# Layer 0's expert stage: first block's rows listed from the ranks, two modulation units moved to the stage's tail

## The chip, the cores and the metric

The kernel runs on one core of one Trainium2 chip, in float32. The metric is device time of one execution in microseconds (us). TensorE (PE, with PEld its weight load), VectorE (DVE), ScalarE (ACT), GpSimd (POOL) and SyncE (SP, which here only issues DMAs) run side by side, each through its own list of instructions in order, and meet at semaphores.

## What is computed

Two model blocks stand one behind the other. The change touches only the first, which has two layers over 512 tokens and 256 context tokens, and in it the end of layer 0: a mixture of experts with 32 experts, two of them chosen for each of the 768 rows, and the modulation vectors with which layer 1 begins.

```python
for layer in range(DEPTH):
    sh1, sc1, g1, sh2, sc2, g2 = jnp.split((silu_c @ mod_w[layer] + mod_b[layer])[:, None, :], N_MOD, axis=-1)
    ...
    h = rmsnorm(x, norm_mix_g[layer]) * (1.0 + sc1) + sh1
    ...
    h2 = rmsnorm(x, norm_ffn_g[layer]) * (1.0 + sc2) + sh2
    ...
        out = hier_moe(jnp.concatenate([h2.reshape(b * s, d), hc2.reshape(-1, d)], axis=0), *moe)
        x = x + g2 * out[: b * s].reshape(x.shape)
```

`hier_moe` picks a group, then two experts in it, sorts the rows by expert, computes `(silu(x @ w_gate[e]) * (x @ w_up[e])) @ w_down[e]` for each expert's rows and adds the weighted results back.

## The kernel before

**One block for each expert.** The 32 experts are given to 32 blocks by rank of their row count. A narrow block holds 64 rows, a wide one 128 (in layer 0 the blocks 7, 14, 21, 26, 4 and 10). Each needs three weight matrices (gate, up, down) of 128 x 4096 float32, 2 MB each. They go round in eight slots: six parts of `ring`, one in `hT`, one in `scr`. Blocks 0 and 1 are always experts of fixed number, so SP can load their weights with plain DMAs before the ranks are known (`fixed` in `sp_moe`); POOL fetches the others with indirect DMAs (`pool_blocks`) whose row numbers stand in `wix`. Should an expert have more rows than its block, further blocks follow in a general path (`further`), which in these runs is branched over.

**The router's stage.** PE multiplies by the router's weights (`pe_router`), DVE finds the two experts of each row, counts, and computes from them where every row goes (`dve_router`). Meanwhile PE transposes the 768 rows of h, ACT copies them to SBUF and POOL writes them as six tiles to `hrows` in DRAM. Then PE turns places into lists (`pe_router_rows`, `pe_router_halves`): for each block the 128 row numbers (`rt`), and where its results go (`rw`, `rn`). DVE signals `order` when the experts' order stands in `wix`, `rt` and `rows` when the lists stand, and `ox` after the tables of the general path and the weights w1, w2. POOL waits for the rows out, for `rt`, gathers the rows of blocks 0 to 2 from `hrows`, waits for `rows`, fetches block 2's gate, waits for `ox`, and then goes through the blocks: rows of b+3, up of b+2, down of b+1, gate of b+3, results of b-1 (to `yrows`). A fetch into a slot waits until PE has done with what was in it.

**Modulation of the next layer.** Units 0 to 3 of layer 1's modulation (2 MB of `mod_w` each) are computed inside layer 0's router stage. SP loads each in two halves of 1 MB into ring slot 0 (`mod_load`); a half waits until PE has done with the half before in its place. PE makes 8 matmuls for a unit (`pe_mod_pieces`), ACT copies the result (`mod_row`), PE turns it into columns (`pe_mod_turn`), ACT copies these (`mod_columns`), and DVE adds the bias. Slot 0 is also the place of block 1's gate, so `fixed(1, 0)` waits for unit 3.

**Layer 1's stage** has no modulation units and already works in another way: DVE makes from block 0's column of the ranks a table `first_oa`, PE multiplies it with the row numbers ("r_0", 4 matmuls there), and `first_rt` lists block 0's rows. POOL gathers them at once, and `pe_router_rows` and `pe_router_halves` stand within block 0's matmuls (`among`, behind steps 2 and 5 of 8).

**The tail.** SP loads the results of six tiles of 128 rows (1 MB each) from `yrows` once all are written, here into ring slots 0 to 2 (`moe_y`). Per tile ACT scales by w1 (`weigh`), DVE and POOL add the second expert's half, PE transposes (`turn`), DVE adds to x (`add`), ACT squares (`squares`), PE sums the squares (`sums`), ACT copies (`groups`), PE makes the total (`total_columns`). Behind it come the root, the reciprocal and layer 1's first scaling.

Of the kernel before, what the change touches and what calls it, by code (L numbers as in the profile page):

```python
# [8 lines left out]
ALU = mybir.AluOpType  # L9
# [17 lines left out]
FIXED = 2  # L27
# [248 lines left out]
def build(nc, I, out, upto=99):  # L276
# [67 lines left out]
    FURTHER_SLOTS = (0, 1, 5, IN_H, IN_SCRATCH, 2)  # L344
# [780 lines left out]
    def expert_slot(kind, b):  # L1125

        if b >= 32:
            return FURTHER_SLOTS[(3 * (b - 32) + kind) % 6]
        read = min(3 * b + 4, 95) if kind == 2 and b < 32 else 3 * b + 4 if kind == 2 else 3 * b - 1 + kind if b else kind
        return EXPERT_SLOTS[read % 8]  # L1130
# [8 lines left out]
    def sp_moe(e, l):  # L1139
# [22 lines left out]
        for u in (1, 2, 3):  # L1162
            mod_load(u)
        fixed(1, *((0, 1) if l == 1 else (1,)))
# [4 lines left out]
        if l == 0:  # L1169
            e.wait_ge(*ps.filled("mod", 1, 3))  # L1170
            fixed(1, 0)
# [29 lines left out]
    def pe_router(e, l):  # L1201
# [45 lines left out]
        if l == 0:  # L1247
            rows(3)
        else:
            o = ps.take("r_0", l)  # L1250
            e.wait_ge(*ps.ready("r_0", l))
            e.wait_ge(*dve_step.of(l, "first_oa"))
            for i in range(NT):
                m = e.matmul(o[:, 0:1], M.first_oa[:, 128 * i:128 * i + 128], k("tok")[:, i:i + 1], i == 0, i == NT - 1)
            m.then_inc(*ps.fill("r_0", l))
# [4 lines left out]
        if l == 0:  # L1260
            for i in range(4, NT):
                rows(i)
# [30 lines left out]
    def act_router(e, l):  # L1293
# [19 lines left out]
        if l == 0:  # L1313
            mod_columns(e, M.mod, 0)
            mod_row(e, M.mod, 2)
            mod_columns(e, M.mod, 1)
            mod_row(e, M.mod, 3)
            mod_columns(e, M.mod, 2)
            mod_columns(e, M.mod, 3)
# [9 lines left out]
    def dve_router(e, l):  # L1329
# [49 lines left out]
        if l == 1:  # L1379
            e.wait_ge(*ps.filled("r_k", l))  # L1380
            rank_in = ps.ap("r_k", l)[:, 0:32 * NT].rearrange("p (t e) -> p t e", e=32)
            chosen = M.AA.rearrange("p (t e) -> p t e", e=32)
            go(e.stt(M.first_key, rank_in[:, :, 0], 1.0, chosen[:, :, 0], ADD, MUL))
            e.stt(M.first_oa.rearrange("p (t s) -> p t s", s=128), M.spread[:, None, :].broadcast_to([128, NT, 128]), 1.0,
# [2449 lines left out]
```

## Time and profile before

| | us |
|---|---|
| median of 3 runs | 2998.05 |
| lowest, highest | 2992.88, 2999.28 |
| the profiled execution: its time | 2988.78 |
| the profiled execution: its span | 2987.0 |
| in it: layer 0's router stage | 288 to 346 |
| in it: layer 0's blocks | 346 to 839 |
| in it: layer 0's tail | 839 to 876 |

All times "at" a point are us from the span's start. The profiled execution is 9.3 us (0.31%) below the median. In a row of the timeline the first number is the start, the second the length, and in brackets stands how long the engine was idle before it and what ended that.

### The profile page before, as it was taken

What the parts mean: (1) busy time and instruction counts of PE and PEld (TensorE: products, weight loads), DVE (VectorE), ACT (ScalarE), POOL (GpSimd) and SP (SyncE); (2) the same over time, 40 slices, a digit from 0 to 9 for tenths busy, and PEclk for the clock granted to TensorE, in tenths of its full rate; (3) what the DMA queues carried; (4) which work ended last, traced back from release to release, by engine and by line L of the source; (5) the groups of instructions that cost most, each with busy time, mean ns of one, the idle gap of its engine ahead of it and who ended that gap; (6) DMA issues with size and microseconds to landing.
All of it is one profiled execution on the core that took longest, in us unless ns stands there. A gap on an engine that the chain in (4) does not pass through costs nothing.

```text
span 2987.0 us, 36438 instructions
## 1 busy us (share of the span) xinstructions
PE 2810.7 (94%) x15530; PEld 1917.0 (64%) x15530; DVE 1045.0 (35%) x2088; ACT 754.0 (25%) x1311; POOL 515.5 (17%) x519
## 2 busy tenths in 40 slices
PE   7989899999979999989999989999999889999997
PEld 4778456544548765745355537888865557888876
DVE  5983300000053343330000016242285554432334
ACT  4142311111142154311111114222111264321223
POOL 0000133332220044133332311000043140000000
PEclk9999899999989999989999999999999999999998
DMA  8612999999942132389999983232311201322321
GB/s 294 200 46 90 385 425 427 426 426 426 412 166 73 57 127 85 122 339 426 426 426 426 426 342 124 87 111 85 127 36 45 103 1 63 117 94 94 99 90 45
DMA packets 142537, 621.51 MB, mean 208 GB/s; under 512 B 15698, under 2 KB 96722, under 8 KB 108704
## 3 DMA queue, kind: packets, MB, share of 16 engines
q0 software_dynamic: 42336, 403.76, 32.1%
q1 hardware_dynamic: 98880, 210.35, 20.4%
q10 hardware_dynamic: 1152, 4.98, 0.5%
q8 instruction: 127, 2.08, 0.3%
q14 instruction: 42, 0.34, 0.0%
HBM read 624.26 MB, written 26.74 MB: 218 GB/s over the span
## 4 chain that ended last, share of the span: by engine, by line
PE 77%; DMA 11%; DVE 5%; ACT 3%; issue 2%; POOL 1%; SPq 1%; DVEq 0%; POOLq 0%; ACTq 0%
PE ps L92 75%; DMA ring<-in_exp_up,wix 7%; PE ps L95 2%; DVE scr L114 2%; ACT hT L98 1%; SPq L132 1%; DMA hT<-in_exp_up,wix 1%; DMA scr<-in_exp_up,wix 1%; DVE xT L114 1%; DMA ring<-in_mod_w 1%; POOL scr L110 0%; DVE scr L117 0%; POOL yrows L139 0%; ACT ring L102 0%; DVE scr L106 0%
## 5 line engine op out<-in xcount | busy, mean ns | idle before, releaser
L92 PE MATMUL ps<-ring_r 128*128 128x512 f32 (+1 forms) x2688 | 772.6, 374 | 6.1 <-DVE hT_r L106 4.0
L92 PEld LDWEIGHTS ps<-ring_r 128*128 128x128 f32 x2688 | 492.7, 190 | 114.0 <-issue 18.3
L92 PE MATMUL ps<-ring,scr 128*64 128x512 f32 (+4 forms) x2176 | 461.2, 548 | 19.4 <-DMA ring<-in_exp_up,wix 14.4
L92 PE MATMUL ps<-hT_r,ring_r 128*128 128x512 f32 (+1 forms) x1256 | 470.0, 374 | 0.0
L92 PEld LDWEIGHTS ps<-ring,scr 128*64 128x64 f32 (+2 forms) x2176 | 163.8, 141 | 223.6 <-issue 210.4
L92 PE MATMUL ps<-scr_r,ring_r 128*128 128x512 f32 x1312 | 306.7, 390 | 0.3 <-issue 0.3
L106 DVE TENSOR_TENSOR scr<-scr,ps 64x512 f32<-64x512 f32 (+1 forms) x76 | 52.5, 691 | 661.4 <-ACT scr L98 498.2
L92 PEld LDWEIGHTS ps<-scr_r,ring_r 128*128 128x128 f32 x1312 | 246.2, 188 | 52.4 <-issue 0.5
L92 PEld LDWEIGHTS ps<-hT_r,ring_r 128*128 128x128 f32 x1256 | 238.4, 190 | 41.2 <-issue 0.5
L92 PE MATMUL ps<-ring,hT 128*64 128x512 f32 (+3 forms) x992 | 247.3, 539 | 16.4 <-DMA ring<-in_exp_up,wix 12.6
L106 DVE TENSOR_TENSOR ring_r<-ring,ring_r 128x2048 fp32r<-128x2048 f32 (+1 forms) x102 | 225.0, 2229 | 89.5 <-ACT ring_r L102 89.2
L102 ACT ACTIVATE ring_r<-ring 128x2048 fp32r<-128x2048 f32 (+1 forms) x102 | 186.5, 1836 | 184.4 <-DMA ring<-in_ffn_w 132.0
L98 ACT ACTIVATE scr<-ps 64x512 f32<-64x512 f32 (+2 forms) x96 | 55.9, 583 | 603.1 <-PE ps L92 603.1
L92 PEld LDWEIGHTS ps<-ring,hT 128*64 128x64 f32 (+1 forms) x992 | 111.4, 166 | 121.9 <-issue 109.3
L92 PEld LDWEIGHTS ps<-KC,scr 128*128 128x128 f32 x1168 | 148.7, 201 | 62.2 <-issue 37.5
L102 ACT ACTIVATE scr<-ps 128x512 f32<-128x512 f32 (+2 forms) x178 | 91.1, 522 | 370.7 <-PE ps L92 367.5
L92 PE MATMUL ps<-KC,scr 128*128 128x64 f32 (+2 forms) x1168 | 156.9, 282 | 23.3 <-DVE scr L106 13.4
L92 PE MATMUL ps<-scr 128*32 128x128 f32 (+5 forms) x712 | 144.5, 409 | 7.9 <-DMA ring<-in_exp_up,wix 3.1
L92 PE MATMUL ps<-ring 128*64 128x128 f32 (+10 forms) x904 | 134.7, 400 | 17.1 <-ACT scr L102 10.1
L103 DVE COPY scr<-ps 128x512 f32<-128x512 f32 (+3 forms) x94 | 46.1, 500 | 290.1 <-PE ps L95 173.6
L92 PE MATMUL ps<-hT,ring 128*32 128x62 f32 (+2 forms) x1088 | 138.6, 316 | 9.2 <-issue 9.2
L106 DVE TENSOR_TENSOR scr<-hT,ps 128x512 f32<-128x512 f32 x44 | 30.2, 687 | 310.3 <-PE ps L92 310.3
(169 smaller groups left out, 2920.0 us busy)
## 6 DMA issues: line engine op xcount, KB each, us to landing
ring<-in_ffn_w SPq DMA_DIRECT2D x66, 1024.0 KB, 5.5
ring<-in_mod_w SPq DMA_DIRECT2D x12, 2048.0 KB, 8.5
ring<-in_mod_w SPq DMA_DIRECT2D x24, 1024.0 KB, 5.7
ring<-in_exp_up SPq DMA_DIRECT2D x4, 2048.0 KB, 11.0
ring<-in_exp_down SPq DMA_DIRECT2D x4, 2048.0 KB, 9.4
ring<-in_exp_gate SPq DMA_DIRECT2D x4, 2048.0 KB, 12.4
ring<-in_w_in SPq DMA_DIRECT2D x4, 2048.0 KB, 8.2
ring<-in_w_cd SPq DMA_DIRECT2D x6, 1024.0 KB, 6.0
```

Source lines behind the costliest of these rows:

```text
L92: return self.real.matmul(o, l, r, start=start, stop=stop) if self.real else Quiet()
L95: return self.real.transpose(o, i, identity) if self.real else Quiet()
L98: return self.real.activation(o, i, f, **how) if self.real else Quiet()
L102: return self.real.activation(o, i, ACT.Copy) if self.real else Quiet()
L103: return self.real.tensor_copy(o, i) if self.real else Quiet()
L106: return self.real.tensor_tensor(o, a, b, op) if self.real else Quiet()
L114: return self.real.scalar_tensor_tensor(out=o, in0=a, scalar=s, in1=b, op0=op0, op1=op1) if self.real else Quiet()
L132: return self.real.dma_start(o, i) if self.real else Quiet()
```

## The change

- Layer 0 also makes `first_oa` and `first_rt` from the ranks (6 matmuls on PE, four operations on DVE); POOL gathers block 0's rows right behind the rows' writes and then fetches block 2's gate at `order`; the lists are made within block 0's matmuls.
- Units 2 and 3 leave the router's stage. Block 1's gate, up are loaded when unit 1 is through.
- The tail's six tiles land in `hT` (2), `scr` (2) and ring slot 2 (2). Units 2 and 3 are loaded whole into ring slots 0 and 1, behind the tail's rows on SP. PE computes them behind tile 4's sums, ACT copies them ahead of tile 5's squares, and DVE's bias and gains stand at the stage's end.
- The general path goes round four slots in place of six.

On SP in layer 0's router stage and behind it (`in_mod_w` 128x2048 is half a unit, 128x4096 a whole one; `w_cd` belongs to layer 1):

```order
 L132 DMA ring<-in_exp_gate 128x4096
-L132 DMA ring<-in_mod_w 128x2048 x6
+L132 DMA ring<-in_mod_w 128x2048 x2
+L132 DMA ring<-in_exp_gate 128x4096
 L132 DMA ring<-in_exp_up 128x4096
-L132 DMA ring<-in_exp_gate 128x4096
 L132 DMA ring<-in_exp_down 128x4096
 L132 DMA ring<-in_w_cd 128x8x256
 L132 DMA ring<-in_w_cd 128x8x128 x2
-L132 DMA ring<-yrows 128x2x1024 x6
+L132 DMA hT<-yrows 128x2x1024 x2
+L132 DMA scr<-yrows 128x2x1024 x2
+L132 DMA ring<-yrows 128x2x1024 x2
+L132 DMA ring<-in_mod_w 128x4096 x2
```

Four half units are gone ahead of the blocks, and two whole units stand behind the six row loads.

On POOL at the start of layer 0's blocks (`scr<-hrows` gathers a block's rows), before:

```order
L132 DMA hrows<-scr 128x1024 x2
L132 DMA hrows<-ring 128x1024 x4
L135 DMA scr<-hrows,scr 128x1024 x3
L135 DMA hT<-in_exp_gate,wix 128x4096
L135 DMA scr<-hrows,scr 128x1024
L135 DMA scr<-in_exp_up,wix 128x4096
```

and in the changed kernel:

```order
L132 DMA hrows<-scr 128x1024 x2
L132 DMA hrows<-ring 128x1024 x4
L135 DMA scr<-hrows,scr 128x1024
L135 DMA hT<-in_exp_gate,wix 128x4096
L135 DMA scr<-hrows,scr 128x1024 x3
L135 DMA scr<-in_exp_up,wix 128x4096
```

Block 2's gate moved ahead of the rows of blocks 1 and 2; the three gathers behind it and block 2's up now wait for lists that PE makes within block 0.

On ACT at the end of the tail (`hT<-xT` are the squares of a tile, `scr<-ps 128x128` the groups), before:

```order
L98 ACTIVATE hT<-xT 128x1024
L102 ACTIVATE scr<-ps 128x128
L98 ACTIVATE hT<-xT 128x1024
L102 ACTIVATE scr<-ps 128x128 x2
L98 ACTIVATE stat<-ps,KC 128x6
```

and in the changed kernel:

```order
L98 ACTIVATE hT<-xT 128x1024
L102 ACTIVATE scr<-ps 128x128
L102 ACTIVATE scr<-ps 128x512 x2
L98 ACTIVATE hT<-xT 128x1024
L102 ACTIVATE scr<-ps 128x128
L102 ACTIVATE MT<-ps 128x8 x2
L102 ACTIVATE scr<-ps 128x128
L98 ACTIVATE stat<-ps,KC 128x6
```

The copies of units 2 and 3 stand ahead of the last tile's squares, the copies of their columns ahead of its groups.

The diff, cut to what the prediction speaks of:

```diff
-    FURTHER_SLOTS = (0, 1, 5, IN_H, IN_SCRATCH, 2)
+    FURTHER_SLOTS = (5, IN_H, IN_SCRATCH, 2)
...
         mod_load(0)
         fixed(0, 0)
-        for u in (1, 2, 3):
-            mod_load(u)
-        fixed(1, *((0, 1) if l == 1 else (1,)))
+        mod_load(1)
+        if l == 0:
+            e.wait_ge(*ps.filled("mod", 1, 1))
+        fixed(1, 0, 1)
...
         e.wait_ge(*xg_in[0].of(l, 0))
-        if l == 0:
-            e.wait_ge(*ps.filled("mod", 1, 3))
-            fixed(1, 0)
         fixed(1, 2)
...
+        for u in (2, 3) if l == 0 else ():
+            weights_load(e, u - 2, ("mod", 1, u), I["mod_w"][1, u], 8, 512)
...
-            pe_mod_pieces(e, 2)
             pe_mod_turn(e, M.mod, 1)
-            pe_router_rows(e, l)
-            pe_mod_pieces(e, 3)
-            pe_router_halves(e, l)
-            pe_mod_turn(e, M.mod, 2)
-            pe_mod_turn(e, M.mod, 3)
...
-        among = {2: pe_router_rows, 5: pe_router_halves} if l == 1 and first == 0 else {}
+        among = {2: pe_router_rows, 5: pe_router_halves} if first == 0 else {}
...
-        if l == 1:
-            e.gather(M.xr[0], hrows, M.first_rt, bounds_check=767, oob_is_err=False).then_inc(*xg_in[0].up(l, 0, by=16))
-            e.wait_ge(*dve_step.of(l, "order"))
-            fetch(FIXED, 0)
+        e.gather(M.xr[0], hrows, M.first_rt, bounds_check=767, oob_is_err=False).then_inc(*xg_in[0].up(l, 0, by=16))
+        e.wait_ge(*dve_step.of(l, "order"))
+        fetch(FIXED, 0)
         e.wait_ge(*dve_step.of(l, "rt"))
-        for b in range(l, 3):
+        for b in (1, 2):
             fetch_x(b)
-        if l == 0:
-            e.wait_ge(*dve_step.of(l, "rows"))
-            fetch(FIXED, 0)
         e.wait_ge(*dve_step.of(l, "ox"))
...
         if l == 0:
-            return ring[:, a:a + 2048]
+            return hT[:, a:a + 2048] if i < 2 else scr[:, a - SLOT:a - SLOT + 2048] if i < 4 else ring[:, a:a + 2048]
...
+        if l == 0:
+            for u in (2, 3):
+                pe_mod_unit(e, M.mod, u)
+            for u in (2, 3):
+                pe_mod_turn(e, M.mod, u)
         sums(M.NT - 1)
...
+            if l == 0 and i == M.NT - 1:
+                mod_row(e, M.mod, 2)
+                mod_row(e, M.mod, 3)
             squares(i)
             if i:
                 groups(i - 1)
+        if l == 0:
+            mod_columns(e, M.mod, 2)
+            mod_columns(e, M.mod, 3)
         groups(M.NT - 1)
...
-        if l == 0:
-            dve_mod_bias(e, M.mod)
-            e.wait_ge(*dve_step.of("mod_b", M.mod.name))
-            dve_gains(e, "at_in", 1, 0, "nmix")
-        else:
+        if l == 1:
             dve_two_gains(e)
```

## Rows read from the trace of the kernel before

**Rows 1.** The page's chain that ended last, by engine.
```profile
PE 77%; DMA 11%; DVE 5%; ACT 3%; issue 2%; POOL 1%; SPq 1%; DVEq 0%; POOLq 0%; ACTq 0%
```

**Rows 2.** Windows: length, PE, PEld, DVE, ACT, POOL busy, PE clock, DMA share, GB/s.
```profile
310.00:330.00 20.00, 15.53 (x126) 11.07 (x125) 16.41 (x62) 9.19 (x19) 3.52 (x6) 1.00 0.83 292
343.00:356.00 13.00, 12.31 (x46) 5.44 (x45) 0.00 (x0) 1.88 (x2) 1.94 (x2) 0.65 1.00 423
372.00:600.00 228.00, 228.00 (x1344) 131.60 (x1344) 20.16 (x34) 26.43 (x45) 72.83 (x75) 1.00 1.01 426
600.00:818.00 218.00, 204.34 (x1124) 105.16 (x1122) 17.36 (x30) 24.99 (x42) 63.15 (x65) 0.98 1.01 424
1302.00:1309.00 7.00, 6.65 (x46) 3.62 (x44) 3.95 (x15) 1.19 (x2) 4.43 (x5) 1.00 0.28 80
```

**Rows 3.** Chain of waits in layer 0's blocks: start, length, what.
```profile
602.41 12.55 PE ps L92 x64
...
619.10 29.06 DMA ring<-in_exp_up,wix
...
794.90 26.92 DMA hT<-in_exp_up,wix
```

**Rows 4.** Timeline of SP and POOL, layer 0's router stage.
```profile
313.35 0.33 SPq L132 DMA_DIRECT2D ring<-in_mod_w  x1
...
335.33 1.09 POOL L135 DMA_INDIRECT scr<-hrows,scr  x1 [9.04 <-DVE scr L106]
...
347.92 0.95 POOL L135 DMA_INDIRECT scr<-in_exp_up,wix  x1 [0.30 <-issue]
```

**Rows 5.** Timeline of POOL, the same place in layer 1.
```profile
1286.83 1.18 POOL L135 DMA_INDIRECT scr<-hrows,scr  x1 [8.77 <-DMA hrows<-ring]
...
1307.25 0.95 POOL L135 DMA_INDIRECT scr<-in_exp_up,wix  x1 [0.30 <-issue]
```

**Rows 6.** Landing of POOL's DMAs issued at 325.8, 1277.5, 360.3, 1311.1.
```profile
DMA to landing us min/median/max: 4.9/4.9/4.9
...
DMA to landing us min/median/max: 8.4/8.4/8.4
...
DMA to landing us min/median/max: 14.1/14.1/14.1
...
DMA to landing us min/median/max: 16.5/16.5/16.5
```

**Rows 7.** Timeline, router lists: PE and DVE in layer 0, then in layer 1.
```profile
328.65 1.83 DVE L106 TENSOR_TENSOR scr<-scr 128x768 f32<-128x768 f32 x2
329.75 3.65 PE L92 MATMUL ps<-scr 128*128 128x49 f32 x24 [1.20 <-DVE scr L106]
335.25 0.72 DVE L117 TENSOR_REDUCE scr<-scr 128x17 f32<-128x544 f32 x1
...
1298.85 1.98 PE L92 MATMUL ps<-scr 128*128 128x43 f32 x16
1302.45 0.52 DVE L117 TENSOR_REDUCE scr<-scr 128x11 f32<-128x352 f32 x1
```

**Rows 8.** The tail's six row loads on SP: issue, and landing.
```profile
L132 SPq DMA_DIRECT2D ring<-yrows x6: 396/516/1060, 843.0 to 846.5; - x6
...
DMA to landing us min/median/max: 6.5/11.6/15.8
```

**Rows 9.** Timeline: unit and turn in the router stage, then the tail's end.
```profile
325.64 1.92 PE L92 MATMUL ps<-ring,scr 128*32 128x512 f32 x16
327.50 1.05 PE L92 MATMUL ps<-AM,scr 128*128 128x2 f32 x8
338.45 0.60 ACT L102 ACTIVATE scr<-ps 128x512 f32<-128x512 f32 x1 [9.69 <-PE ps L92]
...
869.93 1.06 ACT L98 ACTIVATE hT<-xT 128x1024 f32<-128x1024 f32 x1 [0.84 <-DVE xT L114]
871.04 1.08 PE L92 MATMUL ps<-hT,KC 128*32 128x128 f32 x16 [1.02 <-ACT hT L98]
872.05 1.11 PE L92 MATMUL ps<-AM,scr 128*128 128x1 f32 x4
873.92 2.93 PE L92 MATMUL ps<-KC,stat 128*128 128x128 f32 x12 [0.76 <-DVE stat L120]
```

**Rows 10.** Windows at the tail's end, columns as in Rows 2.
```profile
871.00:877.50 6.50, 5.70 (x34) 4.66 (x34) 1.54 (x4) 1.31 (x4) 0.00 (x0) 0.50 0.00 0
```

More of the change, by code:

```diff
@@ L1127, in expert_slot @@
         if b >= 32:
-            return FURTHER_SLOTS[(3 * (b - 32) + kind) % 6]
+            return FURTHER_SLOTS[(3 * (b - 32) + kind) % 4]
         read = min(3 * b + 4, 95) if kind == 2 and b < 32 else 3 * b + 4 if kind == 2 else 3 * b - 1 + kind if b else kind
@@ L1246, in pe_router @@
         e.matmul(o[:, 0:32], k("tri"), M.AA[:, 0:32], True, True).then_inc(*ps.fill("r_k", l))
-        if l == 0:
-            rows(3)
-        else:
[L1250 to L1255, printed above, removed]
+        for i in (3, 4) if l == 0 else ():
+            rows(i)
+        o = ps.take("r_0", l)
+        e.wait_ge(*ps.ready("r_0", l))
+        e.wait_ge(*dve_step.of(l, "first_oa"))
+        for i in range(NT):
+            m = e.matmul(o[:, 0:1], M.first_oa[:, 128 * i:128 * i + 128], k("tok")[:, i:i + 1], i == 0, i == NT - 1)
+        m.then_inc(*ps.fill("r_0", l))
         o = ps.take("r_p", l)
@@ L1260, in pe_router @@
         if l == 0:
-            for i in range(4, NT):
-                rows(i)
+            rows(5)
             pe_mod_turn(e, M.mod, 0)
-            pe_mod_pieces(e, 2)
             pe_mod_turn(e, M.mod, 1)
-            pe_router_rows(e, l)
-            pe_mod_pieces(e, 3)
-            pe_router_halves(e, l)
-            pe_mod_turn(e, M.mod, 2)
-            pe_mod_turn(e, M.mod, 3)
     def pe_router_rows(e, l):
@@ L1378, in dve_router @@
         go(e.reduce(place, cmp, ADD))
-        if l == 1:
[L1380 to L1384, printed above, removed]
-                  bc(M.first_key[:, :, None], 128), ADD, ALU.is_equal).then_inc(*dve_step.up(l, "first_oa"))
+        e.wait_ge(*ps.filled("r_k", l))
+        rank_in = ps.ap("r_k", l)[:, 0:32 * NT].rearrange("p (t e) -> p t e", e=32)
+        chosen = M.AA.rearrange("p (t e) -> p t e", e=32)
+        go(e.stt(M.first_key, rank_in[:, :, 0], 1.0, chosen[:, :, 0], ADD, MUL))
+        e.stt(M.first_oa.rearrange("p (t s) -> p t s", s=128), M.spread[:, None, :].broadcast_to([128, NT, 128]), 1.0,
+              bc(M.first_key[:, :, None], 128), ADD, ALU.is_equal).then_inc(*dve_step.up(l, "first_oa"))
         go(e.ts(cap, rank, WIDES[l] + 0.5, ALU.is_le, 64.0, MUL))
@@ L1396, in dve_router @@
         go(e.ts(rows[:, 128:160], p32(k("iota"))[:, 0:32], p32(k("p")), ALU.is_ge, ov, MUL), l, "by_expert")
-        if l == 1:
-            e.wait_ge(*ps.filled("r_0", l))
-            v = ps.ap("r_0", l)[:, 0:1]
-            go(e.ts(M.first_z, v, 0.5, ALU.is_le, 65536.0, MUL))
-            e.stt(M.first_rt, v, -1.0, M.first_z, ADD, ADD).then_inc(*ps.empty("r_0", l))
+        e.wait_ge(*ps.filled("r_0", l))
+        v = ps.ap("r_0", l)[:, 0:1]
+        go(e.ts(M.first_z, v, 0.5, ALU.is_le, 65536.0, MUL))
+        e.stt(M.first_rt, v, -1.0, M.first_z, ADD, ADD).then_inc(*ps.empty("r_0", l))
         e.wait_ge(*ps.filled("r_p", l))
@@ L1906, in dve_moe @@
         add(M.NT - 1)
+        if l == 0:
+            dve_mod_bias(e, M.mod)
+            e.wait_ge(*dve_step.of("mod_b", M.mod.name))
+            dve_gains(e, "at_in", 1, 0, "nmix")
         stage_end(e, f"m{l}", "act", "pe")
@@ L1913, in pool_moe @@
         e.wait_ge(*rows_out[1].of(l, M.NT - 1))
-        if l == 1:
-            e.wait_ge(*ps.emptied("r_0", l))
+        e.wait_ge(*ps.emptied("r_0", l))
         pool_blocks(e, l)
```

7 lines of the change are left out of this document (removed).

## The prediction

> **What bounds the kernel now.** Start with the chain of waits: 77% of the span is PE's and 11% DMA's [rows 1], so the first reading is that PE decides. In order of time layer 0's blocks look like that too, up to 615; behind it the chain changes to waits for expert weights of 27 to 29 us each [rows 3]. The reader should then turn to the windows, since a chain that runs over PE does not say that the DMA engines had time to spare. From 343 to 818 their share is 1.00 to 1.01 at 423 to 426 GB/s, whether PE waits or not [rows 2]. So the stream of weights is what ends layer 0's blocks. PE has only been given a start by the weights of blocks 0 and 1, and has used it up at 615. The last fetches make it plain: the up weights issued at 794.90 take 26.92 us to land, of which their own 2.10 MB need 2.10/0.426 = 4.92 us; the rest is queue [rows 2, 3]. The time of layer 0's blocks is therefore: the moment from which the stream runs without holes, and what is still to be moved from there. PE's own start is no term as long as the queue stays full. In the tail no DMA queue is full any more; there the last tile's chain from DVE over ACT and PE counts [rows 9].
>
> **The change, part 1: the stream's start.** Removed ahead of the blocks are units 2 and 3, 4.19 MB, worth 4.19/0.426 = 9.8 us of DMA time. What matters is whether holes open instead. I follow the new order.
>
> Block 1's gate and up are issued where unit 2's second half is now, at 313.4 [rows 4], in place of later. That is 4.19 MB, and with the six tiles of `hrows` (3.15 MB) 7.34 MB. At 426 GB/s they take 17.2 us. With some 2 us until the first bytes move (an estimate: half a megabyte alone takes 4.9 us, 1.2 of it bytes [rows 6]) the last row write lands near 313.4 + 2 + 17.2 = 332.6; the stretch ran at 292 GB/s with a share of 0.83, that is 352 at a full share, so I add 0.7: 333.3. The rows' last write itself is hardly moved: `first_oa` (768 columns, 0.92 us [rows 7]) and its matmuls delay the last transposes by a few tenths. The ends: it lands 4.9 us after its issue at 325.8 as now, 330.7; or 8.4 us after as in layer 1, and a bit more for the bigger backlog, 335 [rows 6].
>
> From there layer 1 is the model, because it has this very order. Its last row write lands at 1277.5 + 8.4 = 1285.9 and block 2's up is issued at 1307.25 [rows 5, 6], 21.3 us later: gather of block 0's rows, its transposes, three steps of block 0, the lists, `rt`, the rows of blocks 1 and 2, `ox`, the rows of block 3. Layer 0 has 24 passes for the lists where layer 1 has 16 at 0.124 us (1.98 us), +1.0; and `ox` runs over 17 further blocks instead of 11 in two operations, 0.72 against 0.52 us, +0.4 [rows 7]. So 22.7 us, and the up weights of block 2 go out at 333.3 + 22.7 = 356.0 instead of 347.92 [rows 4]. Before that time POOL has only block 2's gate to fetch and SP only block 1's down, and both have landed by about 348. The DMA engines then run nearly empty, as in layer 1, whose window 1302 to 1309 has a share of 0.28 [rows 2]. The hole eats the 9.8 us.
>
> The balance is read where both stages do the same again, block 3's up. In layer 1 it lands at 1311.1 + 16.5 = 1327.6, 20.3 us after the issue at 1307.25 [rows 5, 6]. Here: 356.0 + 20.3 = 376.3. Now it lands at 360.3 + 14.1 = 374.4 [rows 6]. Behind it the same 86 fetches follow in both kernels. **The stream ends 1.9 us later**; with the ends of the row write -0.7 to +3.6.
>
> What is moved on PE, DVE and ACT here costs nothing of its own: units 2 and 3 (1.92 us each at full clock [rows 9]) leave a stretch in which PE waits for DMA and DVE anyway, and PE reaches block 1 some 2 us earlier than now (an estimate: block 0's rows arrive some 4 us earlier, but the lists, 3 us, stand within its matmuls). That only makes the queue of fetches longer. If the queue were not full, it would be a gain (a rival, below).
>
> **Part 2: the tail.** The six tiles are issued from 843.0 to 846.5, and the last lands 15.8 us after its issue, at 862.3 [rows 8]. The two units are next in SP's queue: 862.3 + 2 x 4.92 = 872.1 for unit 3. All times in this part are those of before; part 1 shifts them together. PE needs 1.92 us for a unit: unit 2 is there early enough and is computed from 870.0, unit 3 is done at 874.1. ACT copies it (0.60, until 874.7), and only then, being in order, squares the last tile, which it now starts at 869.93 although its input is there. Queued behind the waiting ACT instruction is all that the end of the stage needs; who waits for it is PE's last sums. PE meanwhile makes unit 3's turn (1.05, until 876.2 with unit 2's), so the sums that now start at 871.04 start at 876.2 [rows 9]. At full clock they and the last total take some 1.3 us, with ACT's copy between them: 877.5, against 873.2 now (872.05 + 1.11). That is +4.3. One part comes back: sums, totals and roots now run at the level of 0.50, 1.2 GHz, because PE had waited 1.02 us for ACT behind a thin stretch [rows 9, 10]; with the units in that place I expect the 2.4 GHz level to be kept, and the first 8 of 12 root passes (2.93 x 8/12 = 2.0 us) to take half. **+3.4 us**, from +2.5 (unit 3 lands a microsecond earlier) to +9 (clock low, below). DVE's bias and gains (two short operations) are done while ACT and PE make the last total. The landing places in `hT` and `scr` change no length. The third `w_cd` load lands some 10 us later (4.19 MB more ahead of it); it is layer 1's third piece of weights, and PE takes it up only behind two others, so I count it as covered. The general path isn't run; four slots cost nothing.
>
> The Trainium skill, page "TensorE: Matmul & The Clock Gate" (Part 1), says that the throttled state is the default and that activity releases it. By that rule PE's added work before 871 keeps the higher level; the trace of before only shows the fall behind PE's wait, so it does not decide this.
>
> A second rule bears on part 1. The rows show a half-megabyte write of layer 1 landing 8.4 us after its issue while SP's 2 MB loads are ahead of it. The Trainium skill, page "DMA: Bandwidth & Descriptors" (Queues, rings and completion order), says that each DMA engine takes turns between the queue rows, packet by packet. By turns, the last row write would be through once its queue's share is, about a microsecond sooner than with all loads ahead of it, and the stream would end about 1 us later instead of 1.9.
>
> **The sum:** 1.9 + 3.4 = 5.3 us. The profiled execution took 2988.78, so 2994.1; it lies 9.3 us under the median of the three runs, so as a median 2998.05 + 5.3 = **3003.4**.
>
> **Rivals.**
> - **The stream banks all of its 4.19 MB (faster).** Block 2's up would have to be issued when block 1's down lands, near 347, so that no hole opens. Then the stream ends 9.8 us earlier, and with the tail's 3.4 the kernel takes 2991.6. It decides at the issue of that fetch: each microsecond before 354.1 is gained. For it speaks that POOL's first gather comes about 1 us earlier than now (333.3 + 0.9 against 335.33 [rows 4]); against it, that `ox` hangs on block 0's matmuls, and layer 1's hole [rows 2].
> - **PE's chain decides.** If the queue of fetches is not what ends the blocks, PE's earlier start, about 2.2 us, is the gain: -2.2 + 3.4, 2999.3. For it speaks the chain up to 615 [rows 3], against it the share of 1.01 in the same stretch [rows 2].
> - **The low clock in the tail.** If the level falls at 871 as now, units and turns cost double: the two units end at 870.0 + 7.7 = 877.7, turns near 881, the total near 882: +8 to +9 in place of 3.4, 3009. Now the low level holds until 877.5 [rows 10].
> - **The moved units are hidden.** Units 2 and 3 would have to land before 868; they are behind 6.3 MB of rows, so only another order of landing gives it. Price 0 for the tail: 3000.
>
> **Chances.** Forecast 0.50; stream banks 0.11; PE's chain 0.17; low clock 0.16; hidden 0.06. A measurement of this kernel can tell about 0.2%, 6.0 us, from no change. The forecast lies at 5.3 and its own range is 2999 to 3008, so I count 0.22 of its 0.50 as slower and 0.28 as same; low clock is slower (0.15); half of the first rival is faster (0.06), with 0.03 for starts that I have not seen. Faster 0.09, same 0.53, slower 0.38. The range is 2991 to 3011: from the first rival to low clock with the late row write.
>
> **What would show it.** In the trace of after: the last row write lands near 333; block 0's gather behind it by 1 us; block 2's up issued near 356 (this decides part 1); a window of low DMA share from 348 to 357; block 3's up lands near 376; from there all transfers shifted by 2 us; in the tail unit 3's matmuls wait for DMA until 872 plus the shift, ACT's squares of the last tile start near 875 plus the shift, and PE's clock is 1.00 there. I am wrong if the window near 350 is full, if the last up lands earlier than now, or if squares are not late.

## The result

| | before | after |
|---|---|---|
| median, lowest to highest (10 runs each) | 2993.62 (2988.20 to 2999.28) | 3002.76 (2997.61 to 3009.56) |
| the profiled execution: time, span | 2988.78, 2987.0 | 3000.24, 2998.5 |
| first scaling of layer 1 in it | 876.11 | 883.53 |

All in us. The changed kernel is slower: ratio 1.0031, 95% interval 1.0023 to 1.0040, that is 9.3 us (6.9 to 12). The three runs shown ahead of the prediction had a median of 2998.05; with ten it is 2993.62. In the two profiles the stage of the change ends 7.4 us later. The rest of the gap of 11.5 us between the two spans arises in code that the change doesn't touch (see the last section).

The profile after. The page's chain of waits by engine, against [rows 1]:

```profile
PE 70%; DMA 12%; ACT 2%; issue 2%; DVE 2%; POOL 1%; DVEq 0%; SPq 0%; POOLq 0%; ACTq 0%
```

Windows of the changed kernel; the columns are those of [rows 2] (the last two numbers are the DMA share and GB/s, ahead of them the PE clock):

```profile
300.00:330.00 30.00, 26.53 (x172) 17.33 (x170) 20.40 (x73) 14.94 (x30) 3.51 (x6) 0.88 0.85 334
330.00:345.00 15.00, 4.58 (x20) 4.00 (x21) 1.93 (x3) 1.48 (x3) 2.09 (x2) 0.50 0.71 268
345.00:365.00 20.00, 18.99 (x102) 9.38 (x100) 5.43 (x20) 1.76 (x3) 6.85 (x7) 0.88 0.57 211
...
350.00:360.00 10.00, 9.33 (x67) 6.04 (x67) 5.00 (x19) 0.68 (x2) 3.45 (x4) 1.00 0.21 62
...
372.00:600.00 228.00, 228.00 (x1346) 131.59 (x1342) 20.21 (x34) 26.21 (x44) 72.42 (x75) 1.00 1.01 426
```

And the same three first stretches of the kernel before:

```profile
300.00:330.00 30.00, 23.64 (x178) 14.16 (x177) 20.23 (x70) 15.42 (x31) 3.52 (x6) 1.00 0.89 338
330.00:345.00 15.00, 13.82 (x74) 10.24 (x73) 5.14 (x20) 0.95 (x3) 4.06 (x4) 0.55 0.99 395
345.00:365.00 20.00, 19.02 (x85) 7.69 (x85) 1.12 (x2) 3.07 (x4) 4.82 (x5) 0.82 1.01 429
```

This is the reading that decides the case. Before, the DMA engines are busy all the time from 330; after, they stand nearly still from 350 to 360, and are idle for about three tenths of 330 to 345. From 372 the stream is full in both kernels, so hardly anything behind it can make the hole good (about a microsecond was, see the prediction's steps). A stream that always ends the stage may be accounted like money: share times length is the time for which the engines were busy. From 300 to 380 the kernel before uses 76.9 us of full share, the changed one 62.7 us. It loses 14.2 us, has 9.8 us less to move, and should end 4.4 us later. The chain of waits of the changed kernel, against [rows 3], shows its last fetches:

```profile
621.70 31.52 DMA ring<-in_exp_up,wix
...
797.42 28.71 DMA hT<-in_exp_up,wix
...
852.07 23.73 DMA ring<-in_mod_w
```

Start plus length is the landing: the one issued at 797.42 lands at 826.13, before at 794.90 + 26.92 = 821.82. That is 4.3 us later, as the account says. The third row is new: the tail now ends on the landing of unit 3.

Why the hole is there, from POOL's timeline after, against [rows 4]:

```profile
328.25 0.53 POOL L132 DMA_DIRECT2D hrows<-ring  x1 [4.65 <-ACT ring L102]
336.58 1.09 POOL L135 DMA_INDIRECT scr<-hrows,scr  x1 [7.80 <-issue]
337.98 1.00 POOL L135 DMA_INDIRECT hT<-in_exp_gate,wix  x1 [0.30 <-issue]
354.38 1.00 POOL L135 DMA_INDIRECT scr<-hrows,scr  x1 [15.41 <-DVE scr L103]
...
359.55 0.95 POOL L135 DMA_INDIRECT scr<-in_exp_up,wix  x1 [0.30 <-issue]
```

POOL waits 15.41 us for the lists (DVE's copy into `scr`), with only block 2's gate in its queue, which landed at 349.4; SP has only block 1's down, landed at 352.0. Block 2's up, which before went out at 347.92, goes out at 359.55. What POOL waits for is on PE:

```profile
325.96 1.12 PE L95 MATMUL ps<-KC,hT 128*128 128x128 f32 x4 [1.46 <-DVE scr L106]
...
344.38 5.39 PE L92 MATMUL ps<-ring,hT 128*64 128x512 f32 x12 [0.73 <-issue]
349.69 2.96 PE L92 MATMUL ps<-scr 128*128 128x49 f32 x24
```

The lists (x24) stand behind 5.39 us of block 0's matmuls, which run at the low level behind a wait of 9.68 us for block 0's rows (the window 330 to 345 has a clock of 0.50, and so has 326 to 330 ahead of the wait); the next 12 take 2.80. The first row shows a smaller thing: the last transposes of h wait 1.46 us for DVE, since they take the PSUM bank in which the ranks stood. DVE in turn makes `first_oa` (0.96 us) ahead of the sums for PE's next product. So the last row write goes out at 328.25 and not at 325.77. Whether that costs anything is tested below ("The last transposes").

The tail after, PE and then ACT and DVE, against [rows 9]:

```profile
873.17 1.92 PE L92 MATMUL ps<-ring,scr 128*32 128x512 f32 x16
875.84 1.92 PE L92 MATMUL ps<-ring,scr 128*32 128x512 f32 x16 [0.75 <-DMA ring<-in_mod_w]
877.70 1.95 PE L92 MATMUL ps<-AM,scr 128*128 128x2 f32 x16
879.57 0.65 PE L92 MATMUL ps<-hT,KC 128*32 128x128 f32 x16
...
881.82 2.46 PE L92 MATMUL ps<-KC,stat 128*128 128x128 f32 x12 [0.76 <-DVE stat L120]
```

```profile
877.83 0.60 ACT L102 ACTIVATE scr<-ps 128x512 f32<-128x512 f32 x1 [2.08 <-PE ps L92]
878.33 1.05 ACT L98 ACTIVATE hT<-xT 128x1024 f32<-128x1024 f32 x1
...
883.53 2.97 DVE L114 SCALAR_TENSOR_TENSOR hT<-xT,AM,ps 128x512 f32<-128x512 f32 x5 [1.77 <-PE ps L92]
```

Unit 3's matmuls wait for its landing (875.80), ACT copies it, and only then makes the squares of the last tile. From the first row load to the first scaling the tail takes 883.53 - 847.04 = 36.5 us, before 876.11 - 843.04 = 33.1: 3.4 us more. Its PE clock is 1.00 where [rows 10] had 0.50:

```profile
871.00:877.50 6.50, 4.98 (x54) 1.80 (x53) 2.11 (x9) 1.82 (x3) 0.00 (x0) 1.00 0.91 338
```

### The profile page after: what moved, and what is told of

It is laid out like the page before. It is cut to its first block, busy times and chain, and to the rows that moved or that the text cites. A ratio compares the mean times of both kernels' runs of the same rounds, so it can differ in the third digit from the quotient of the medians.

```text
span 2998.5 us, 36465 instructions
## 1 busy us (share of the span) xinstructions
PE 2812.2 (94%) x15542; PEld 1918.3 (64%) x15542; DVE 1046.8 (35%) x2092; ACT 755.1 (25%) x1311; POOL 516.9 (17%) x519
## 3 DMA queue, kind: packets, MB, share of 16 engines
q1 hardware_dynamic: 98592, 210.35, 20.3%
## 4 chain that ended last, share of the span: by engine, by line
PE 70%; DMA 12%; ACT 2%; issue 2%; DVE 2%; POOL 1%; DVEq 0%; SPq 0%; POOLq 0%; ACTq 0%
PE ps L92 67%; DMA ring<-in_exp_up,wix 7%; PE ps L95 2%; DMA hT<-in_exp_up,wix 2%; ACT hT L98 1%; DMA scr<-in_exp_up,wix 1%; DMA ring<-in_mod_w 1%; POOL yrows L139 0%; POOL scr L110 0%; DMA scr<-hrows,scr 0%; ACT ring L102 0%; ACT scr L102 0%; DMA hrows<-ring 0%; POOL scr L135 0%; POOL ring L110 0%
## 6 DMA issues: line engine op xcount, KB each, us to landing
ring<-in_exp_gate SPq DMA_DIRECT2D x4, 2048.0 KB, 11.1
```

## The experiments

The theory to be tested was by now: **two bills**. The lists within block 0 open a hole that costs more than the units' 9.8 us bring, and the tail pays 3.4 us for unit 3's late landing. "Row load" below is the start of the tail's first row load on SP (before 843.04), "scaling" the first scaling of layer 1 (before 876.11). All such landmarks stand on one profiled execution each, and kernels with the same instructions up to a landmark differ there by a microsecond or two: the row load came at 843.04 and 841.93 with before's instructions, at 847.04 and 845.70 with the changed kernel's. The ratios come from 5 to 12 runs.

**The units alone.** Units 2 and 3 go to the tail as in the change; block 0's rows and the lists stay as before.

```diff
             for i in range(4, NT):
                 rows(i)
             pe_mod_turn(e, M.mod, 0)
-            pe_mod_pieces(e, 2)
             pe_mod_turn(e, M.mod, 1)
             pe_router_rows(e, l)
-            pe_mod_pieces(e, 3)
             pe_router_halves(e, l)
-            pe_mod_turn(e, M.mod, 2)
-            pe_mod_turn(e, M.mod, 3)
...
```

> Units 2 and 3 in the tail as in the changed kernel, but layer 0's lists made ahead of block 0 and POOL's order as before. Theory (the hole): what costs time in the changed kernel is that the lists stand within block 0's matmuls, so that block 2's up (issued at 359.6 there, 347.9 before) and block 3's gate wait while the DMA engines run empty. Then here the up goes out near 346, block 3's up lands near 367 instead of 374.5 (before) and 379.8 (changed), the blocks end some 6 us earlier than before, the tail gives 3 to 4 us back, and the kernel takes about 2991. Rival (the writes): the whole shift of 5 us is that the last row write lands at 335.7 instead of 330.7, behind 4.2 MB of gate and up loads. Those are here too, so the stream would end 4 to 5 us later than before and the kernel would take 3001 to 3003.

Measured: 2993.92, ratio 1.0004 (0.9995 to 1.0013). Row load 838.69, scaling 875.32.

```profile
330.00:345.00 15.00, 9.38 (x44) 8.67 (x46) 4.76 (x20) 1.23 (x2) 4.51 (x5) 0.50 0.62 216
345.00:365.00 20.00, 19.66 (x97) 9.01 (x94) 1.81 (x3) 2.42 (x4) 5.31 (x6) 0.90 1.01 423
```

No hole from 345 on, but one from 330 to 345. Of the 9.8 us the stream banks 4.4 us, where the expectation had 6, and the tail takes 3.5 us of them back (36.6 against 33.1). The time lies 3 us above the 2991 expected; the rival's 3001 to 3003 is excluded.

**The first block alone.** The kernel before with `first_oa`, `first_rt` and the lists within block 0; all four units stay.

```diff
...
-        among = {2: pe_router_rows, 5: pe_router_halves} if l == 1 and first == 0 else {}
+        among = {2: pe_router_rows, 5: pe_router_halves} if first == 0 else {}
...
```

> Block 0's rows from the ranks and the lists within block 0, but units 2 and 3 stay in the router stage. Theory (the hole): block 2's up still waits for the lists, near 360, and only the backlog of loads fills part of the hole; block 3's up lands near 379, 5 us later than before, and with the tail unchanged the kernel takes 2998 to 3000. Rival (the writes): the row writes are not behind early gate and up loads, so nothing is late and the kernel takes 2992 to 2995.

Measured: 2999.43, ratio 1.0015 (1.0005 to 1.0025). Row load 854.28, scaling 886.97.

```profile
345.00:365.00 20.00, 18.62 (x93) 11.35 (x93) 4.99 (x19) 2.65 (x4) 2.75 (x3) 0.73 0.79 322
```

```profile
334.26 1.00 POOL L135 DMA_INDIRECT hT<-in_exp_gate,wix  x1 [0.30 <-issue]
360.38 1.00 POOL L135 DMA_INDIRECT scr<-hrows,scr  x1 [25.13 <-DVE scr L103]
```

POOL's wait for the lists is 25.13 us here, because PE still makes units 2 and 3 ahead of block 0 (with waits of 1.59 and 2.60 us for their loads): the lists come at 355.77, 6.1 us later than in the changed kernel, and block 2's up goes out at 365.54, where the expectation had 360. The time lies in the range expected and excludes the rival. The profiled stage says more than the time: it ends 10.9 us late, and the median is 4.5 us (1.5 to 7.5) up. This profiled execution was the slowest of the kernel's 11, 6.5 us above their median; how much of that lies in this stage stays open.

**The lists ahead of block 0.** The changed kernel with one edit: the lists are made before block 0's matmuls again.

```diff
             rows(5)
             pe_mod_turn(e, M.mod, 0)
             pe_mod_turn(e, M.mod, 1)
+            pe_router_rows(e, l)
+            pe_router_halves(e, l)
...
-        among = {2: pe_router_rows, 5: pe_router_halves} if first == 0 else {}
+        among = {2: pe_router_rows, 5: pe_router_halves} if l == 1 and first == 0 else {}
```

> The changed kernel with one edit: PE makes the lists (pe_router_rows, pe_router_halves) ahead of block 0, in the time in which it waits for block 0's rows. Theory (the hole): the last row write stays at 335.7, but rt is there near 336 and ox near 341, block 2's up goes out near 345 instead of 359.6, block 3's gate near 354 instead of 360.8, block 3's up lands near 368 instead of 379.8, and the kernel takes about 2992, 10 to 11 us less than the changed one. Rival (the writes): the row write is as late as in the changed kernel, so only the 3 us of list matmuls within block 0 are saved: 2999 to 3003.

Measured: 2993.69, ratio 1.0001 (0.9991 to 1.0011), 9 us below the changed kernel and in the range expected. Row load 837.34, scaling 874.41.

```profile
345.49 0.95 POOL L135 DMA_INDIRECT scr<-in_exp_up,wix  x1 [0.30 <-issue]
```

```profile
330.00:345.00 15.00, 10.62 (x49) 9.52 (x50) 6.58 (x21) 1.76 (x3) 4.89 (x5) 0.50 0.69 259
345.00:365.00 20.00, 19.66 (x102) 9.38 (x100) 1.81 (x3) 2.07 (x5) 5.41 (x7) 0.92 1.01 415
```

Block 2's up goes out at 345.49 in place of 359.55, and the second hole is closed. Of the change's two parts it is the place of the lists that makes it slow.

The account of the stream for all of these, from the four windows 300 to 330, 330 to 345, 345 to 365 and 365 to 380 (us of full share used; "less" is against before; the last column is measured):

| kernel | used | less | units gone | stream should end | row load came |
|---|---|---|---|---|---|
| before | 76.9 | | | | |
| after | 62.7 | 14.2 | 9.8 | +4.4 | +4.0 |
| units alone | 70.8 | 6.1 | 9.8 | -3.7 | -4.4 |
| first block alone | 67.1 | 9.8 | 0 | +9.8 | +11.2 |
| lists ahead | 71.8 | 5.1 | 9.8 | -4.7 | -5.7 |
| transposes sooner (below) | 64.3 | 12.6 | 9.8 | +2.8 | +3.0 |

Five kernels agree with it to 1.5 us, which is what landmarks scatter by. PE's own progress tells the sign but not the size: its first matmul with block 1's weights comes 1.7 us later than before in the changed kernel (360.61 against 358.94), 2.4 sooner with the units alone, 7.7 later with the first block alone and 3.0 sooner with the lists ahead, each time 0.4 to 0.7 of the row load's shift.

**The tail in another order.** The changed kernel, with the last tile's squares and sums ahead of unit 3's copy.

```diff
+            pe_mod_unit(e, M.mod, 2)
         sums(M.NT - 1)
         total_columns(M.NT - 2)
         total_columns(M.NT - 1)
+        if l == 0:
+            pe_mod_unit(e, M.mod, 3)
+            for u in (2, 3):
+                pe_mod_turn(e, M.mod, u)
...
```

> The changed kernel with the tail's order mended: PE makes the last tile's sums and totals between unit 2 and unit 3, ACT squares the last tile ahead of the copies. Theory (the order): the cost of the tail is half that the last squares stand behind unit 3's copy; with the sums done before unit 3 lands only unit 3, its turn and the roots are behind it, and layer 1's first scaling starts 2 us earlier than in the changed kernel (883.5 there): 3000 to 3001. Rival (the landing decides alone): unit 3's landing at 875.8 and the work behind it set the end in either order; nothing changes, 3002 to 3003.

Measured: 3003.47, ratio 1.0043 (1.0029 to 1.0057). Row load 845.70, scaling 882.45: 36.75 us, not shorter. The squares now start at 872.2, unit 3 lands at 874.5, and the last total is made at 875.45.

```profile
875.38 1.92 PE L92 MATMUL ps<-ring,scr 128*32 128x512 f32 x16
879.97 0.27 ACT L98 ACTIVATE stat<-ps,KC 128x6 f32<-128x6 f32 x1 [0.58 <-DVEq L143]
```

The 2 us expected did not come, but the rival "the landing decides alone" is not shown either. PE comes to unit 3 only behind the totals, 0.9 us after its landing, and the root (the second row), which needs only the totals, still stands behind unit 3's columns and DVE's gains, 4.5 us after the last total. From the root's start to the first scaling it takes another 2.5 us. An order with the root ahead of unit 3's columns was not tried; so how much of the tail's 3.4 us is the landing's and how much the order's stays open.

**Four slots only.** The kernel before with the general path on four slots.

```diff
-    FURTHER_SLOTS = (0, 1, 5, IN_H, IN_SCRATCH, 2)
+    FURTHER_SLOTS = (5, IN_H, IN_SCRATCH, 2)
```

> The kernel before with four slots in the general path, nothing else. The general path is branched over in these runs, so every theory expects the time of before within 0.1% (within 3 us), and stage landmarks as before: rows of the tail requested near 843, first scaling of layer 1 near 876. If it is slower by 3 us or more, the list of slots counts after all, through code or addresses, and the sums of the other runs must be made again.

Measured: 2994.34, ratio 1.0008 (0.9996 to 1.0021). No difference that can be told; scaling 874.88.

**The last transposes without the bank's wait.** The changed kernel with tile 3's transposes ahead of the counting matmuls.

```diff
-        for i in range(3 if l == 0 else NT):
+        for i in range(4):
             rows(i)
...
-        for i in (3, 4) if l == 0 else ():
+        for i in (4,) if l == 0 else ():
             rows(i)
```

> The changed kernel with the transposes of tile 3 of h in front of the counting matmuls, so that tile 5's second half no longer takes the PSUM bank of the ranks and does not wait for DVE to read them. Theory 'the bank's wait delays the writes': last row write issued near 326 in place of 328.2, landed near 333.5 in place of 335.7, block 2's up weights issued about 2 us earlier than 359.6, stage end about 2 us earlier, about 3001. Rival 'the backlog of loads sets the landing': the last write lands at 335 to 336 however early it is issued, and nothing after it moves: the time of the changed kernel, about 3003.

Measured: 2999.93, ratio 1.0036 (1.0021 to 1.0052). Row load 846.0, scaling 882.53, 1.0 us before the changed kernel's.

```profile
323.91 1.97 PE L95 MATMUL ps<-KC,hT 128*128 128x128 f32 x8
```

```profile
335.81 1.09 POOL L135 DMA_INDIRECT scr<-hrows,scr  x1 [8.23 <-issue]
```

The wait on PE is gone (eight transposes in one piece). The last write goes out 1.2 us sooner (327.05), block 0's gather starts 0.8 us sooner. But SP issued block 1's gate 0.9 us sooner too in this execution, and that accounts for all of it, as four executions show:

| kernel | block 1's gate issued | last row write issued | landed | landing behind the gate's issue |
|---|---|---|---|---|
| changed | 314.24 | 328.25 | 335.7 | 21.4 |
| transposes sooner | 313.36 | 327.05 | 334.9 | 21.5 |
| lists ahead | 313.62 | 328.21 | 335.3 | 21.7 |
| lists ahead, transposes sooner, units early (below) | 313.60 | 326.10 | 335.2 | 21.6 |

In the last two the write goes out 2.1 us apart and lands within 0.2 us. So the rival is right in its mechanism: the backlog of loads and writes sets the landing, and the bank's wait costs nothing here. The 1.0 us at the stage's end is within what landmarks of equal code scatter by.

**The units' loads ahead of the last expert weights.** The changed kernel; units 2 and 3 are loaded as soon as their slots are free and computed before the rows come.

```diff
+        for u in (2, 3) if l == 0 else ():
+            weights_load(e, u - 2, ("mod", 1, u), I["mod_w"][1, u], 8, 512)
         e.wait_ge(*expert_there(l, 2, 31))
...
```

> The changed kernel with units 2 and 3 loaded when the last expert weights are through, ahead of the rows of the tail, and computed in front of them. Theory 'the tail pays for their landing behind the rows': their 9.8 us of transfers fit between the last fetch, landed at 836, and the first rows, requested at 847, so the tail is as long as before (33 us from the first row load to the first scaling, in place of 36.5) and the time is 3.5 us lower, 2999 to 3000. Rival 'the transfers only move the bill': rows, results or layer 1's first pieces of weights come later by as much, and the time stays at 3001 to 3004.

Measured: 3010.94, ratio 1.0065 (1.0053 to 1.0077), the slowest of all. Scaling 891.71.

```profile
816.67 5.85 SPq L132 DMA_DIRECT2D ring<-in_mod_w  x2
...
855.16 0.91 SPq L132 DMA_DIRECT2D hT<-yrows  x2
```

The row load comes 8.1 us after the changed kernel's 847.04. The slots were free at 816, when the last expert weights were still on their way, so 4.19 MB went into a full queue and were paid nearly in full. The expectation put them behind the last fetch, which the edit does not do; its rival, at 3001 to 3004, was too low as well. And the tail still took 36.6 us, now because ACT's copies of the units held back its first scaling of a tile until 865.35, 4.5 us after the first rows had landed at 860.86.

**The same with the lists ahead and the transposes sooner.** The three edits together.

```diff
+        for u in (2, 3) if l == 0 else ():
+            weights_load(e, u - 2, ("mod", 1, u), I["mod_w"][1, u], 8, 512)
         e.wait_ge(*expert_there(l, 2, 31))
...
+            pe_router_rows(e, l)
+            pe_router_halves(e, l)
...
```

> The changed kernel with three things undone or moved: the lists ahead of block 0, tile 3's transposes ahead of the counting matmuls, units 2 and 3 loaded ahead of the tail's rows. If the hole in the stream and the tail are separate and add, the first row load of the tail comes near 837 (as in the run with the lists ahead) or 835 with the earlier writes, the tail takes 33 us, and the stage ends 6 to 8 us before that of the kernel before: 2986 to 2989, faster than both. Rival: the earlier end of the blocks is lost again because the two units collide with the last fetches or results: 2992 to 2995.

Measured: 3000.78, ratio 1.0021 (1.0009 to 1.0034). Row load 846.76, against 837.34 with the lists ahead alone: 9.4 us for 9.8 us of transfers. The expectation (2986 to 2989) failed by the same step, and its rival (2992 to 2995) priced the collision too low.

**Unit 2 in the gap ahead of the rows.** Here it stands behind the last fetch and layer 1's first pieces of weights; unit 3 stays behind the rows. With the lists ahead:

```diff
             early_load(e, key)
+        if l == 0:
+            weights_load(e, 0, ("mod", 1, 2), I["mod_w"][1, 2], 8, 512)
         e.wait_ge(*y_out[0].of(l, 30))
...
-        for u in (2, 3) if l == 0 else ():
-            weights_load(e, u - 2, ("mod", 1, u), I["mod_w"][1, u], 8, 512)
+        if l == 0:
+            weights_load(e, 1, ("mod", 1, 3), I["mod_w"][1, 3], 8, 512)
...
```

> The changed kernel with the lists ahead of block 0, and unit 2 loaded ahead of the tail's rows but behind layer 1's first pieces (not ahead of the last expert weights, as in the run before); unit 3 stays behind the rows, and its copy on ACT goes behind the last squares. With the lists ahead the first row load came at 837.3, 5.7 us before that of the kernel before, and the DMA engines had nothing to do from about 832. Theory 'two separate bills': unit 2 fits in that gap, unit 3 lands 4.9 us earlier than the 866.0 of the run with the lists ahead, the tail takes 33 to 34 us as in the kernel before, and the first scaling of layer 1 comes near 871, 5 us earlier than 876.1: 2987 to 2990, faster than both. Rival 'whatever stands ahead of the rows is paid in full': the first row load comes 4 us later, the tail starts later, and the time is that of the run with the lists ahead or worse, 2993 to 2997.

Measured: 2988.82, ratio 0.9985 (0.9975 to 0.9994). That is the time expected, but not the way: the row load came at 843.62, not 837, and the scaling at 875.53, not 871. A time that agrees while its landmarks don't proves nothing, so kernel and control were run again:

> The same kernel as e11 (lists ahead, unit 2 ahead of the rows), run again beside e14. In its first profile the first row load did not come at 837 but at 843.6 and the first scaling of layer 1 at 875.5, only 0.6 us before that of the kernel before, while the time was 4.7 us lower. Theory 'the stage gives half a microsecond, the rest is scatter of the clock in later stages': the time comes out between 2990 and 2994 this time. Rival 'the gain is real and comes again': 2987 to 2990, and the profile shows where.

> The same kernel as e3 (the changed kernel with the lists ahead of block 0), run again on the chip of e13. Its first scaling of layer 1 came 1.7 us before that of the kernel before, and its time equalled that of before within 3 us. Both theories expect 2991 to 2995 again; if e13 is faster than it by 3 us or more, unit 2's place is worth that, wherever it shows.

Measured: 2991.65, ratio 0.9995 (0.9984 to 1.0005), and for the control 2993.27, ratio 1.0000 (0.9991 to 1.0008). The gain did not come again. SP in the repeat, and then in the control:

```profile
828.23 2.91 SPq L132 DMA_DIRECT2D ring<-in_mod_w  x1
841.15 0.91 SPq L132 DMA_DIRECT2D hT<-yrows  x2
...
844.61 1.02 SPq L132 DMA_DIRECT2D ring<-in_mod_w  x1
```

```profile
837.21 0.91 SPq L132 DMA_DIRECT2D hT<-yrows  x2
```

Unit 2 ahead of the rows delays them by 3.9 us (841.15 against 837.21). The tail behind them is shorter by 4.4 us (31.9 against 36.3), scaling 873.06 against 873.55. What stands ahead of the rows is paid there, what stands behind them is paid in the tail.

**The same edit with the lists within block 0:**

> The changed kernel with the same edit of the tail alone (unit 2 ahead of the rows, unit 3's copy behind the last squares); the lists stay within block 0. Theory 'two separate bills': the first row load near 847.0 as in the changed kernel, the tail 33 to 34 us in place of 36.5, first scaling near 880.5 in place of 883.5: 3 us under the changed kernel, 2998 to 3000, still slower than before by the stream's 4 us. Rival: the tail stays at 36 to 37 us because ACT or PE loses at its start what it gains at its end: 3001 to 3004.

Measured: 3001.21, ratio 1.0030 (1.0019 to 1.0041). Row load 851.17, 4.1 us after the changed kernel's; scaling 883.16 against 883.53. The time is the rival's, the way is not: the tail is 32.0 us, even shorter than the theory had it, and it is the row load that comes later by what the tail gains.

No version tried beats the kernel before in a way that came again. The changed kernel with the lists ahead of block 0 equals the kernel before in time.

## The prediction, step by step

**What bounds the kernel** held: the account above is this statement with numbers. By the rival "PE's chain decides" the lists' place would have been worth what PE gains by it, 4.7 us (block 1 from 355.94 in place of 360.61); the row load moved by 9.7 us and the time by 9. The side statement that PE would reach block 1 some 2 us earlier was wrong: PE took up block 0's rows 2.2 us earlier, not 4, and with the lists in between and the first steps at the low clock it came to block 1 1.7 us later.

**The last row write** was the step that failed most. Forecast 333.3 with ends 330.7 to 335; measured 335.7. The forecast added bytes to SP's issue at 313.4, and that is the right mechanism; the two terms were too small. The issue came at 314.24, since PE's second half of unit 1 ran partly at the low level in this execution (1.93 us against 1.07 before; in the other executions above it came at 313.4 to 313.6). And the landing came 21.4 us behind it in place of 19.9, in all four executions of the table above within 0.3. The issue of the last write, which the forecast put "a few tenths" later and which came 2.5 us later (328.25 for 325.77), did not matter, so that its landing 7.4 us behind that issue, for 7.5 forecast, is chance.

```profile
hrows<-ring POOLq DMA_DIRECT2D x1, 512.0 KB, 7.4
...
scr<-in_exp_up,wix POOLq DMA_INDIRECT x1, 8.9
...
ring<-in_exp_up,wix POOLq DMA_INDIRECT x1, 16.5
```

These are the landings (last number) of the DMAs issued at 328.25, 359.55 and 363.37. The first five row writes of the changed kernel landed 11.1 to 12.8 us after their issue, the first of them at 329.62, together with block 1's up (329.61), which SP had issued 2.6 us earlier; before, with units' halves of 1 MB beside them, the six took 3.0 to 7.5 us. The Trainium skill, page "DMA: Bandwidth & Descriptors" (Queues, rings and completion order), says that each DMA engine takes turns between the queue rows, packet by packet. The trace agrees. These are packets and MB of SP's queue and of POOL's from 322 to 322.5:

```profile
q1 hardware_dynamic: 11, 0.16, 81.3%
q0 software_dynamic: 12, 0.05, 23.8%
```

From 322 to 327 it is 104 packets of SP's queue and 105 of POOL's, but 1.62 MB against 0.43: a packet of the loads carries 16 KB (a row of 4096 elements), one of the writes 4 KB (1024 elements). Equal turns gave the writes a fifth of the bytes until the loads were through, and after that the writes had the engines to themselves. The forecast's own use of the rule, a landing a microsecond sooner, did not come.

**From there to block 2's up**: forecast 22.7 us after layer 1's model, measured 359.55 - 335.66 = 23.9. The difference is block 0's first steps, which ran at the low level: 5.39 us for 12 matmuls that took 4.17 us in the model (layer 1 of the kernel before, at 1294.75). Forecast 356.0, measured 359.55.

**The stream's end**: forecast +1.9 with ends to +3.6, measured +5.4 at block 3's up (363.37 + 16.5 = 379.9 against 374.4) and +4.3 at the last fetch. Mechanism right, hole found where forecast (348 to 357; measured 350 to 360, share 0.21), its size too small by 3.5 us: 2.4 from the row write, 1.2 from the way to block 2's up. The last link was exact (20.3 us from that issue to block 3's up). From there to the last fetch 1.1 us were made good; the stream ran at 426 GB/s from 600 to 818 where before it ran at 424, which over 218 us is 1.0 us.

**The tail**: forecast +3.4, measured +3.4. The links up to the squares came as told: last row landed at 865.44, unit 3 at 875.80 (10.4 us behind it for a forecast of 9.8), squares at 878.33. Behind them two misses cancel, which is luck. Counted from the row load, the last total is made 3.9 us later than before, for 4.3 forecast, and the roots give back 0.5 us, not 1.0: the clock was 1.00 up to 882, but 0.50 again from 883 to 885, while the root passes ran. The Trainium skill, page "TensorE: Matmul & The Clock Gate" (Part 1), says that activity releases the throttle; from 871 to 877.5, with the units in that place, the clock is 1.00 where it was 0.50 before, which agrees. The forecast also named ACT's order as what holds back the sums. The reordered tail, which was no shorter, does not settle whether that order or the landing costs the 3.4 us.

**The sum**: 5.3 forecast, 7.4 at the stage's end, 9.3 (6.9 to 12) in the medians. The time lay at 3002.76 for a forecast of 3003.4 because the start was too high by 4.4 us, a median of three, and the step too low by 3.8. That the time came within a microsecond is luck: two errors of opposite sign. "Slower" had 0.38 and "same" 0.53; with the true size of the hole it would have been the other way round.

**The rivals.** The first rival's price does not follow from its own rule: each microsecond before 354.1 gained makes 7.1 us at 347, not 9.8; with the lists ahead the fetch went out at 345.49, 8.6 us before that point, and the row load gained 5.7. The stream banks a part of its 9.8 us only without the lists in block 0: 4.4 us with the units alone, 5.7 with the lists ahead, since the hole from 330 to 345 stays. Of that the tail takes 3.5 us or more back, and the rest (0.8 and 1.7 us) can't be told in the times. The low clock in the tail did not come.

## What to carry to other kernels

Where a transfer queue ends a stage, account its busy share times length over the start: every microsecond in which it has nothing to do is paid at the end (within 1.5 us in five kernels here), and a transfer taken out is worth its bytes only if the next one can be issued in its place. Work that produces addresses (here the lists) belongs ahead of all work that only consumes, even if an engine waits for the latter. And a place is no gap because one queue is quiet there: what was put ahead of a load that someone waits for was paid nearly in full (3.9 and 4.1 of 4.9 us, 8.1 and 9.4 of 9.8). Last, two queues that take turns by packets share the bytes by the size of their packets.

## What the runs showed beside

- **An order of instructions does not show who owns a bank, and a wait that the trace shows need not cost anything.** A transposition in a fixed order waited 1.46 us for a bank eight takes old, whose last reader had just been made later. The write behind it went out later by that and landed no later, since the queue was full.
- **POOL paces the tail.** Its two operations for a tile come every 2.97 us (here tiles 2 and 3 of the changed kernel: 858.83, 861.80), while rows land every 2.5 us (852.72, 855.24, 857.77). So later tiles could probably land a little later without loss; no run tests that.

```profile
858.83 1.57 POOL L110 TENSOR_SCALAR scr<-scr 128x512 f32<-128x512 f32 x1
860.55 1.28 POOL L106 TENSOR_TENSOR scr<-scr 128x512 f32<-128x512 f32 x1
```

- **The clock scatters in code that is the same.** In the second model block the changed kernel's profile loses a further 3.7 us. The window 2370 to 2500 of before and after:

```profile
2370.00:2500.00 130.00, 111.36 (x873) 73.87 (x873) 67.69 (x334) 78.83 (x245) 49.62 (x96) 0.95 0.07 24
```

```profile
2370.00:2500.00 130.00, 109.03 (x1036) 70.33 (x1036) 66.31 (x332) 76.82 (x244) 49.92 (x96) 0.89 0.06 20
```

The granted clock is 0.95 and 0.89, with four slots only 0.92, with unit 2 in the gap (its first run) 0.95. The windows lie at the same times, so up to 11.5 us apart in the program. Between two loads of SP that stand in all four (`in_cmp_w` near 2333, `in_w_out` near 2492) it takes 159.50, 163.20, 162.56 and 159.62 us in this order: the four-slot kernel, whose executed work is that of before, loses 3.1 us there too. So a difference of 3 to 4 us between two profiled spans says little about a change at 350; the landmarks of the stage, which came again within 0.9 us in the control (scaling 874.41 and 873.55) and within 2.5 us in the kernel with unit 2 in the gap (875.53 and 873.06), say more. The same warns of intervals: 0.9975 to 0.9994 was followed by 0.9984 to 1.0005 for one and the same kernel.
